# Seven block products in place of eight for two row pairs of the first gate and value chunks

## The reference, cut to what matters

```python
h = rms_norm(x, norm_mix_g)          # x: 256 x 2048
z = h @ w_in                         # w_in: 2048 x 9280
u_conv, c_q, c_kv, k_pe, gate_logits = split(z)
a, gate = split(u_conv)              # 2048 columns each
u = a * sigmoid(gate)                # then a causal convolution over the tokens, 31 taps
...
cos, sin = rope_tables(positions)    # used on q_pe and k_pe much later
```

## Time and profile before

| what | us |
|---|---|
| median of 3 runs | 1595.68 |
| the profiled execution | 1594.99 |
| its span, first to last instruction | 1592.7 |
| TensorE busy in it | 1581.0 |
| VectorE busy | 1309.1 |
| ScalarE busy | 902.9 |
| POOL busy | 94.2 |

### The profile page before, as it was taken

The page is one execution under the profiler, slowest core; times in us unless marked ns, Lnnn a source line. Parts: engine busy times, 40 slices in busy tenths (PEclk is TensorE's granted clock), DMA queues, the critical chain, the costliest instruction groups (busy, mean ns, idle before and its releaser), DMA issues.

```text
span 1592.7 us, 22193 instructions
## 1 busy us (share of the span) xinstructions
PE 1581.0 (99%) x7909; PEld 1341.3 (84%) x7909; DVE 1309.1 (82%) x1757; ACT 902.9 (57%) x1138; POOL 94.2 (6%) x174
## 2 busy tenths in 40 slices
PE   9999999999999999999999999999999999999997
PEld 7888888888888888888888888888888888888886
DVE  5588999999998998787997786886779776978687
ACT  7444456555555556754566666455655565546655
POOL 6500010000000000000000000000000000000001
PEclk9999999999999999999999999999999999999999
DMA  7666655655655666657664676888678867887694
GB/s 259 200 189 186 192 160 177 175 181 172 185 174 174 209 201 185 197 177 243 216 197 146 184 228 185 281 261 289 180 259 266 271 212 221 281 272 225 205 295 147
DMA packets 169581, 336.68 MB, mean 211 GB/s; under 512 B 10377, under 2 KB 23297, under 8 KB 169089
## 3 DMA queue, kind: packets, MB, share of 16 engines
q1 hardware_dynamic: 164608, 324.84, 65.0%
q0 software_dynamic: 4864, 10.80, 3.1%
q10 hardware_dynamic: 32, 0.01, 0.0%
HBM read 326.16 MB, written 2.10 MB: 206 GB/s over the span
## 4 chain that ended last, share of the span: by engine, by line
PE 98%; DVE 0%; ACT 0%; issue 0%; ACTq 0%; POOL 0%; POOLq 0%; DVEq 0%
PE ps L2566 15%; PE ps L1979 12%; PE ps L1981 12%; PE ps L1980 12%; PE ps L2257 9%; PE ps L2259 9%; PE ps L2258 9%; PE ps L2568 7%; PE ps L1992 1%; PE ps L2168 1%; PE ps L2393 1%; PE ps L2163 1%; PE ps L2146 1%; PE ps L2148 1%; PE ps L2147 1%; PE ps L2202 1%
## 5 line engine op out<-in xcount | busy, mean ns | idle before, releaser
L717 ACT ACTIVATE w_both<-raw 128x1024 fp32r<-128x1024 f32 x522 | 550.6, 1059 | 488.1 <-PE ps L1981 176.4
L1213 DVE TENSOR_TENSOR w_both<-raw,w_both 128x1024 fp32r<-128x1024 f32 x522 | 634.8, 1223 | 192.5 <-ACT w_both L717 190.4
L2566 PE MATMUL ps<-a_both,w_both 128*128 128x512 f32 x1024 | 321.6, 395 | 0.0
L1979 PE MATMUL ps<-w_both,a_both 128*128 128x512 f32 (+1 forms) x636 | 251.3, 395 | 0.1
L1981 PE MATMUL ps<-w_both,a_both 128*128 128x512 f32 (+1 forms) x636 | 247.0, 388 | 0.0
L1980 PE MATMUL ps<-w_both,a_both 128*128 128x512 f32 (+1 forms) x636 | 247.0, 388 | 0.0
L2568 PEld LDWEIGHTS ps<-a_both,w_both 128*128 128x128 f32 x1024 | 192.4, 188 | 45.4
L1274 DVE SCALAR_TENSOR_TENSOR acc<-hconv,cwk,acc 128x256 f32<-128x256 f32 x464 | 201.3, 488 | 7.7 <-PE ps L2202 7.6
L2568 PE MATMUL ps<-a_both,w_both 128*128 128x256 f32 x1024 | 201.1, 278 | 0.0
L2257 PE MATMUL ps<-w_both,c_hi 128*128 128x512 f32 x402 | 156.8, 390 | 0.0
L2259 PE MATMUL ps<-w_both,c_lo 128*128 128x512 f32 x402 | 156.4, 389 | 0.0
...
## 6 DMA issues: line engine op xcount, KB each, us to landing
raw<-in_w_ff_dram SPq DMA_DIRECT2D x225, 512.0 KB, 4.6
raw<-in_w_in_dram SPq DMA_DIRECT2D x137, 512.0 KB, 3.9
...
raw<-in_w_mla_out_dram SPq DMA_DIRECT2D x32, 512.0 KB, 4.3
raw<-in_w_conv_out_dram SPq DMA_DIRECT2D x32, 512.0 KB, 4.4
raw<-in_w_out_dram SPq DMA_DIRECT2D x32, 512.0 KB, 4.5
raw<-in_w_ukv_dram SPq DMA_DIRECT2D x16, 512.0 KB, 3.8
raw<-in_w_xkv_dram SPq DMA_DIRECT2D x16, 512.0 KB, 4.0
```

The lines of the kernel that those rows point to most:

```text
L717: act.activation(whi[:, s, :], raw[:, s, :], ACT.Copy).then_inc(hi_ready, 1)
L1213: dve.tensor_tensor(wlo[:, s, :], raw[:, s, :], whi[:, s, :].bitcast(F32), ALU.subtract).then_inc(lo_ready, 1)
L1979: pe.matmul(sum_, x_hi[:, k0 + k, tok], w_hi, start=(first and k == 0), stop=False)
L2566: pe.matmul(both, whi[:, s, cols[n]], a_both[:, :, k0 + k, :], start=(first and k == 0), stop=False)
```

## The change

Row pairs 6 and 7 (row tiles 12 to 15) of the first gate and value chunks take seven block products. The sixteen units of both chunks are now one list, `E_UNITS`: gate 0 to 5, value 0 and 1, left 0, right 0, value 2 and 3, left 1, right 1, value 4 and 5. "left m" is 6 matmuls and "right m" 15, which wait for the sums of weight blocks (`t_lo_ready`) and of activation blocks (`eh_lo_ready`). The sums of weight blocks need their own copy of the four blocks (`e_raw`, 1 MB per pair, two DMAs behind the loads of units 6 and 9). The last `turn_out` copies its four row tiles twice (to `a_hi` and to `e_act`). The sums of squares move behind `hi(10)`, the transposes of vectors and convolution weights behind both chunks, and the sigmoid acts on a sum in SBUF in place of PSUM. POOL starts the rotary angles when both pairs are through (`m_done`). Cut to its core (left out: buffers, semaphores, the offsets of counts in the feed-forward):

```diff
 X_BEFORE, X_AFTER = (1, 3, 5), (2, 4, 6)
+EM = 2
+E_PLAIN = KT - 2 * EM
+E_UNITS = ([("gate", m) for m in range(E_PLAIN // 2)]
+           + [("value", 0), ("value", 1), ("left", 0), ("right", 0), ("value", 2), ("value", 3), ("left", 1), ("right", 1), ("value", 4), ("value", 5)])
+E_LOAD = {6: 0, 9: 1}
+E_M1, E_M7, E_M6, E_M5 = 4, 5, 6, 7
...
-            for k in range(1, UPC):
-                load(U_CONV + k, 0, w_in[:, 2 * k:2 * k + 2, COL_G:COL_G + NC])
-                if k in (1, 2, 4):
-                    load_x((1, 2, 4).index(k) + 1)
-            load_chunk(U_CONV + UPC, 0, w_in, COL_A)
+            for n in range(1, 2 * UPC):
+                kind, m = E_UNITS[n]
+                if kind == "gate":
+                    load(U_CONV + n, 0, w_in[:, 2 * m:2 * m + 2, COL_G:COL_G + NC])
+                elif kind == "left":
+                    load(U_CONV + n, 0, w_in[:, E_PLAIN + 2 * m:E_PLAIN + 2 * m + 2, COL_G:COL_G + NC])
+                elif kind == "right":
+                    load_second(U_CONV + n, 0, w_in[:, E_PLAIN + 2 * m + 1, COL_A:COL_A + NC])
+                else:
+                    load(U_CONV + n, 0, w_in[:, 2 * m:2 * m + 2, COL_A:COL_A + NC])
+                if n in (1, 2, 4):
+                    load_x((1, 2, 4).index(n) + 1)
+                if n in E_LOAD:
+                    j = E_LOAD[n]
...
+                    kts = slice(E_PLAIN + 2 * j, E_PLAIN + 2 * j + 2)
+                    sp.dma_start(e_raw[j % SLOTS][:, B11:B21 + 1:2, :], w_in[:, kts, COL_G:COL_G + NC]).then_inc(t_landed[j % SLOTS], 16)
+                    sp.dma_start(e_raw[j % SLOTS][:, B12:B22 + 1:2, :], w_in[:, kts, COL_A:COL_A + NC]).then_inc(t_landed[j % SLOTS], 16)
...
+            pool.wait_ge(m_done, EM)
             pool.wait_ge(pos_landed, 16)
             step(pool.tensor_copy(hi_p[:, 0:TT], pos_i[:]))
...
-            for k in range(1, UPC):
-                hi(U_CONV + k)
-                if k in X_AFTER:
-                    c = X_AFTER.index(k) + 1
-                    turn_out(T_X + c, a_hi, CPB * c, V_MIX)
-            square_sums(sq_x, x_in, ss_x)
-            hi(8)
-            act.wait_ge(ss_ready, SS_X)
-            root(sd_x, ss_x, D)
-            for k in range(6, 2 * UPC):
-                hi(U_CONV + k + LEAD)
-                if k == 9:
-                    act.wait_ge(used, U_CONV + UPC)
-                    act.wait_ge(rs_ready, R_X)
-                    glu_gate()
+            def turn_out_whole(c):
+
+                for b in range(2):
+                    act.wait_ge(turned, 2 * (T_X + c) + b + 1)
+                    for dst, k0 in ((a_hi, 0), (e_act, E_PLAIN)):
+                        for k in range(CPB * c + 2 * b, CPB * c + 2 * b + 2):
+                            last = act.activation(dst[:, k - k0, :], ps[:, 6 + b, SEQ * (k % 2):SEQ * (k % 2 + 1)], ACT.Copy,
+                                                  scale=vec[:, V_MIX + k:V_MIX + k + 1])
+                    last.then_inc(turn_hi, 1)
...
+            for n in range(1, 2 * UPC + LEAD):
+                if n < 2 * UPC and E_UNITS[n][0] == "right":
+                    hi_second(U_CONV + n, 0)
+                else:
+                    hi(U_CONV + n)
+                if n in X_AFTER:
+                    c = X_AFTER.index(n) + 1
+                    if CPB * c >= E_PLAIN:
+                        turn_out_whole(c)
+                    else:
+                        turn_out(T_X + c, a_hi, CPB * c, V_MIX)
+                if n == 8:
+                    eh_high(0)
+                    e_high(0)
+                if n == 12:
+                    e_high(1)
+                if n == 10:
+                    for t in range(TT):
+                        wait(act, ss_ready, t)
+                        act.activation(sq_x[:], x_in[:, t, :], ACT.Square, accum_out=ss_x[:, t:t + 1]).then_inc(ss_ready, 1)
+                    act.wait_ge(ss_ready, SS_X)
+                    root(sd_x, ss_x, D)
+                if n == 16:
+                    act.wait_ge(used, U_CONV + 2 * UPC - 3)
+                    act.activation(rows[:, 1, 0, :], ps[:, E_M1, :], ACT.Copy).then_inc(em_copied, 1)
+            act.wait_ge(sg_ready, 1)
+            act.wait_ge(rs_ready, R_X)
+            for t in range(TT):
+                last = act.activation(rows[:, 1, t, :], rows[:, 1, t, :], ACT.Sigmoid, scale=rs_x[:, t:t + 1])
+            last.then_inc(em_copied, 1)
...
+            def eh_sums(half):
+
+                dve.wait_ge(turn_hi, 2 * (T_X + E_PLAIN // CPB + half + 1))
+                blocks = e_act[:, 4 * half:4 * half + 4, :].rearrange("p (m k) (t s) -> p m k t s", k=2, t=TT)
+                x11, x12, x21, x22 = (blocks[:, :, k, t, :] for t, k in ((0, 0), (0, 1), (1, 0), (1, 1)))
+                s1, s2, s3, s4 = (eh_sum[half][:, i, :, :] for i in range(4))
+                dve.tensor_tensor(s1, x22, x21, ALU.subtract).then_inc(eh_made, 1)
+                dve.tensor_tensor(s3, x11, x21, ALU.subtract).then_inc(eh_made, 1)
+                dve.wait_ge(eh_made, 4 * half + 1)
+                dve.scalar_tensor_tensor(out=s2, in0=s1, scalar=-1.0, in1=x11, op0=ALU.mult, op1=ALU.subtract).then_inc(eh_made, 1)
+                dve.wait_ge(eh_made, 4 * half + 3)
+                dve.tensor_tensor(s4, x12, s2, ALU.add).then_inc(eh_made, 1)
...
+            def e_sums(j):
+
+                t = e_raw[j % SLOTS]
+                dve.wait_ge(t_landed[j % SLOTS], 32 * (j // SLOTS + 1))
+                dve.tensor_tensor(t[:, T1:T3 + 1, :], t[:, B11:B12 + 1, :], t[:, B12::2, :], ALU.add).then_inc(t_made, 1)
+                dve.wait_ge(t_made, 3 * j + 1)
+                dve.tensor_tensor(t[:, T2, :], t[:, B22, :], t[:, T1, :], ALU.add).then_inc(t_made, 1)
+                dve.wait_ge(t_made, 3 * j + 2)
+                dve.tensor_tensor(t[:, T4, :], t[:, B21, :], t[:, T2, :], ALU.add).then_inc(t_made, 1)
...
+            def em_sums():
+
+                both, minus = rows[:, 1, :, :], rows[:, 0, :, :]
+                dve.wait_ge(em_copied, 1)
+                dve.wait_ge(m_done, EM)
+                dve.tensor_tensor(both, ps[:, 2:4, :], both, ALU.add).then_inc(sg_ready, 1)
...
+            for n in range(1, 2 * UPC + LEAD):
+                if n == 2 * UPC + 1:
+                    em_sums()
+                if n < 2 * UPC and E_UNITS[n][0] == "right":
+                    lo_second(U_CONV + n, 0)
+                else:
+                    lo(U_CONV + n)
+                if n in X_AFTER:
+                    c = X_AFTER.index(n) + 1
                     turn_low(T_X + c, a_lo, a_hi, CPB * c, V_MIX)
-            lo(8)
-            for k in range(6, 2 * UPC):
-                lo(U_CONV + k + LEAD)
-                if k == 8:
+                if n == 7:
+                    eh_sums(0)
+                    e_sums(0)
+                if n == 8:
+                    eh_low(0)
+                if n == 9:
+                    e_low(0)
+                if n == 11:
+                    e_sums(1)
+                if n == 12:
                     reciprocal(rs_x, sd_x, R_X)
-                if k == 10:
-                    dve.wait_ge(vec_turned, 2)
-                    dve.tensor_copy(vec[:, KT:], ps[:, 5, KT:V_N]).then_inc(vec_ready, 1)
-                    dve.wait_ge(cw_turned, 1)
-                    dve.tensor_copy(cw[:].rearrange("p k s -> p (k s)"), ps[:, 4, :]).then_inc(conv_step, 1)
+                if n == 13:
+                    e_low(1)
             dve.wait_ge(used, U_CONV + 2 * UPC)
-            dve.wait_ge(sg_ready, 1)
+            dve.wait_ge(em_made, 4)
+            dve.tensor_tensor(rows[:, 0, :, :], ps[:, 0:2, :], rows[:, 0, :, :], ALU.add).then_inc(em_made, 1)
+            dve.wait_ge(em_made, 5)
+            dve.wait_ge(em_copied, 2)
             dve.wait_ge(rs_ready, R_X)
-            glu()
+            for t in range(TT):
+                last = dve.scalar_tensor_tensor(out=rows[:, 0, t, :], in0=rows[:, 0, t, :], scalar=rs_x[:, t:t + 1],
+                                                in1=rows[:, 1, t, :], op0=ALU.mult, op1=ALU.mult)
+            last.then_inc(chunk_out, 1)
+            dve.wait_ge(vec_turned, 2)
+            dve.tensor_copy(vec[:, KT:], ps[:, 5, KT:V_N]).then_inc(vec_ready, 1)
+            dve.wait_ge(cw_turned, 1)
+            dve.tensor_copy(cw[:].rearrange("p k s -> p (k s)"), ps[:, 4, :]).then_inc(conv_step, 1)
...
+                kind, m = E_UNITS[n]
+                left, right = E_PLAIN + 2 * m, E_PLAIN + 2 * m + 1
+                if kind == "gate":
+                    pe.wait_ge(turn_lo, n + 1)
+                pe.wait_ge(lo_ready, U_CONV + n + 1)
+                if kind == "gate":
+                    for k in range(2):
+                        for t in range(TT):
+                            mm = product(2 + t, *tokens(2 * m + k, t), *e_slot(n, k))
+                    mm.then_inc(used, 1)
+                elif kind == "left":
+                    pe.wait_ge(turn_lo, left // 2 + 1)
```

(58 more changed lines are left out.)

51 lines of the change are left out of this document (37 added, 14 removed).

## The result

The changed kernel takes 1602.24 us (median of 6 runs, 1602.14 to 1602.65), the kernel before 1595.86 beside it (6 runs, 1595.43 to 1596.12): ratio 1.0041, 95% interval 1.0028 to 1.0054. It is slower by 6.4 us. The prediction said 1602.7, from 1599.8 to 1606.5, with 0.90 for slower: the way and the size are right.

A forecast was written before the change was run, and what follows sets the result against it. TensorE, busy 1581.0 of 1592.7 us, was taken to bound the kernel. About 8.4 us of new waits, with six matmuls fewer, made net +7.0 on 1595.68: 1602.7 us, range 1599.8 to 1606.5.

The forecast's parts named there:

- What is taken away: TensorE, first chunks: two pairs of 24 matmuls become 21, six fewer at 0.227, saving 1.36 us.
- The chain to left 0: VectorE makes seven sums to 33.4, then unit 8's low part to 34.6; TensorE, due at 32.39, waits 2.2 us.
- Right 0: Weight high part to 35.3, low part to 38.9; TensorE's last twelve matmuls from 39.0, about 2.3 us more waiting.
- Unit 11: Its low part follows the squares and root, ready at 44.8 where TensorE wants it at 44.55: 0.3 us wait.
- The second pair: A chain of ScalarE and VectorE; TensorE starts its twelve matmuls at 53.0 instead of 44.65: 8.4 us waits in all.
- Unit 16: Start of the unit after both chunks and transposes: at 62.6 where it was 55.58, +7.0 us.
- The loads at nothing: SP queue: 0.75 MB more per pair, costing nothing; unit 8 lands by 27.6 and VectorE reaches it at 33.4.
- The rotary move at 0 us: POOL's angles moved later give VectorE nothing, since POOL yields: low part 1226 ns with or without them; 0 us.
- The rule that stood beside this step: Trainium skill: VectorE and GpSimd arbitrate for one port pair, loser blocks fully; if VectorE lost, silent POOL would shorten its sums.
- 1: All low parts and sums hide under TensorE, decided at unit 8; not slower, 1594.3 us; chance 0.05.
- rival 2: Only the first pair waits, the second pair's sums running early: waits 4.5, net +3.1, 1598.8 us; chance 0.08.
- 3: The clock falls to 1.2 GHz in TensorE's gaps at the pairs, adding 2.4 to 5.4: about 1606 us; chance 0.12.

The follow-up runs named there:

- experiment 1: Changed kernel with the rotary angles started on POOL as early as before the change: 1602.8 us, ratio 1.0045.
- Experiments 4 and 5: Changed kernel, squares moved, products taking parts of x without sums: 1595.9 us; the same with the second block's load behind unit 11's: 1594.36 us.
- experiments 1 and 8: Rotary angles back at their early place on POOL: in the changed kernel 1602.8 us, in the kernel with its side work spread 1595.44 us.
- experiment 3: Changed kernel with the squares and the root moved to where ScalarE idled: 1598.96 us, ratio 1.0024.
- experiment 2: Changed kernel with the low part of unit 8 ahead of the seven sums on VectorE: 1603.38 us, ratio 1.0049.

## Why the prediction held

- **What is taken away**, 1.36 us: held. The run without sums reaches unit 16 1.52 us before the kernel before, with a time 1.2 us lower.
- **The chain to left 0**: sums to 33.4, low part of unit 8 at 34.6, a start 2.2 us late; measured 33.35, 34.49 and 34.54 - (32.25 + 0.227) = 2.06.
- **Right 0**: weight high part to 35.3, low part to 38.9, start at 39.0; measured 35.30, 38.74 and 38.89.
- **Unit 11**: 0.3 of waiting expected. TensorE started at 44.56 where 44.45 was due: 0.1, no bracket.
- **The second pair**: start of the twelve at 53.0, measured 52.54; it is 7.8 us behind the 44.74 that 54 matmuls from 32.48 would give, 8.4 were forecast. The difference is high part 11, forecast to end at 43.55 and out when VectorE takes it at 43.28, and short steps behind it.
- **Unit 16** at 62.6, +7.0: measured 62.14, +6.56, and the median +6.4. The profiled run itself is 7.65 above that of before; 0.66 of the difference arises between unit 16 and the last matmul, 0.40 of it a wait near 790 us in a far later stage, which the trace of experiment 1, with the same chunks, does not have.
- **The loads at nothing**: right for the changed kernel, and for the reason given, that VectorE was later anyway. Experiments 4 and 5 measure what lay under this cover: 1.8 us, for the second block. My arithmetic was on the first block's load; it was the second's that came out.
- **The rotary move at 0 us**: the one step that failed, by 0.7. It read the median of 1226 ns beside POOL as "POOL yields" and passed over the maximum of 1322 in the same row; three of those thirteen low parts were longer than the rest (1258, 1253 and 1322). In experiments 1 and 8 the median itself is 1305 and 1337. The rule that stood beside this step spoke for a gain, and the runs gave it. Why the kernel before has only these three is open; VectorE idled more in it (busy 17.11 of 30 us, against 25.21). It did not reach the sum: the chain was priced with the feed-forward's durations, which agree with the changed kernel's, where POOL is silent.
- **The rivals**: 1 fell at the place named, unit 8. 2 fell because e_sums(1) did stand behind the squares; experiment 3 is rival 2 made by hand, at 1598.96 where 1598.8 was worked out. 3 did not happen in the profiled execution of the changed kernel, whose longest gap is 1.90, and did in experiment 2; there a fall at the first pair was absorbed wholly, where I had allowed for part. It may have come in other executions of the changed kernel: the mean granted clock over the span is 0.998 in the profiled one, 0.995 in the one with the fall in experiment 2, and 0.995 and 0.996 in two of the six of the changed kernel, at 1602.18 and 1602.65 us, within 0.5 of the fastest (1602.14). No trace of these two shows it; if it came, the waits of the second pair took it up there too.
